# Three attentions of a fused two-block transformer: their steps ordered in pairs on TensorE, ScalarE and VectorE

## The chip, the cores and the metric

The kernel runs on one core of one Trainium2 chip, as one launch. The metric is the device time of that launch in microseconds (us). The core has five engines that run their own instruction streams and meet at semaphores: TensorE (PE; its weight loads are shown apart as PEld), VectorE (DVE), ScalarE (ACT), GpSimd (POOL) and SyncE (SP), which here only issues DMAs.

## What is computed

Two transformer blocks in float32 on one sequence of 512 tokens with a width of 1024. The first has a sparse attention over selected keys (a), a squared-relu MLP, a forgetting attention (b) and a second MLP; the second block has a grouped-query attention (c), an MLP, a chunked gated MLP and a last MLP. Cut to the three attentions, with 16 heads of 64:

```python
# a: keys of each query chosen by an indexer; 4 key/value heads for 16 query heads
p = jax.nn.softmax(jnp.where(valid, q @ k_sel.T * scale, -jnp.inf)); o = p @ v_sel
# b: causal, 16 key/value heads, with a decay added to the scores
p = jax.nn.softmax(jnp.where(causal, q @ k.T * scale + decay, -jnp.inf)); o = p @ v
# c: all 512 keys, 4 key/value heads, normed and rotated queries and keys
p = jax.nn.softmax(q @ k.T * scale); o = p @ v
```

Each o is multiplied by an output weight and added to the residual.

## The kernel before

The program is written engine by engine (`tensor_program`, `scalar_program`, `vector_program`, `gpsimd_program`, `sync_program`), each in the order in which its engine executes it. There is no scheduler: what stands first in a function is issued first, and an engine that waits for a semaphore holds everything written behind it. The activations lie transposed (width on the partitions, tokens along the free dimension). Float32 accuracy in the large matmuls comes from a split of both operands into a high and a low part: `Xhi`, `Xlo` for the activations, `whi`, `wlo` for the weights.

An attention is 32 steps. `STEPS` (line 358) lists them: step n is the pair of heads c = n // 4 and the block of 128 queries i = n % 4. In a and b a block sees only the keys up to its own, so a step's width w is 128, 256, 384 or 512 in turn (`width`, line 362); in c it is always 512. A step has two rows, r = 2n and r = 2n + 1, one for each head. The work of a step, and the lines of it:

- scores (L666, in b with a second product behind it, L674): one product of queries and keys for each head, each in a PSUM bank of its own (`score_bank`: banks 0 to 3, two steps in turn);
- VectorE takes both rows out of PSUM into `PROBS`, with scale or mask and the row's extreme (L1534 in c, L1536 in a and b);
- ScalarE takes the exponential in place and sums it (L1120);
- VectorE inverts both sums of the step (L1549) and multiplies one row in four by its factor (L1552); GpSimd multiplies the other three (L1947);
- turning (L694): TensorE transposes the two rows, in blocks of 64 by 128, into banks 4 and 5;
- the two banks are copied to `TURNED`, of which there are three: of four rows ScalarE copies three (L1114) and VectorE the fourth, row 0 of each even step (L1543);
- values (L711): TensorE multiplies the turned rows with v into bank 6 or 7, one for each pair of heads in turn;
- after four steps the bank holds a chunk of the result; ScalarE writes its high part `Xhi` (L1124), then VectorE the low part `Xlo` (L1556), which waits for `Xhi`. `VALUED` (line 355) says at which n of the loop that is done: 12, 16, 20, ..., 36 and 38.

The steps are staggered. TensorE's loop (`steps`, lines 715 to 722) does at n the scores of n, the turning of n - 4 (`TURN`) and the values of n - 6 (`SUM`). ScalarE's (`attend`, L1103) does at n the copies of turning n - 4 and then both exponentials of n. VectorE's (`attend`, L1519) does at n the score rows of n, at even n the copy of turning n - 4, then the factors of n - 1, and `Xlo`. GpSimd's follows the factors in the order of the steps.

What waits for what, among these: the turning of n waits until both banks of turning n - 1 have been copied (`tr_act`, `tr_dve`), and for its scaled rows (`pn_dve`, `pn_pool`). The scores of n wait until VectorE has taken out the scores of n - 2 (`sc_out`), which had the same banks. The values of n wait for the copies of turning n, and at the first step of a pair of heads also for an earlier `Xlo`, whose bank they reuse (lines 705 and 706). VectorE's score rows of n wait for turning n - 5, which frees their place among the ten rows of `PROBS` (`ROWS`). The first four steps of b are done between the tiles of the product before it, and those of c likewise; the other 28 steps of each attention stand alone. A product with `Xhi` and `Xlo` follows each attention (L531 to L533).

Of the kernel before, what the change touches and what calls it, by code (L numbers as in the profile page):

```python
# [133 lines left out]
def body(nc, ctx, t, consts, out):  # L134
# [289 lines left out]
    def tensor_program(pe):  # L424
# [225 lines left out]
        def attention(a, last, heads_q, heads_k, heads_v):  # L650

            base, x0 = 64 * ATT[a], fill_base(a + "o")[1]
            end = GEMM[last].end

            def scores(n):
                c, i = STEPS[n]
                w = width(a, i)  # L660
                for e in range(2):
                    if TURN <= n < TURN + 2:
                        pe_until.wait_ge(*freed(end - 4 + (score_bank(n, e) - end) % 4))
                    elif n >= 2:
                        pe_until.wait_ge(sc_out, base + 2 * n + e - 3)
                    m = pe.matmul(bank[score_bank(n, e)][:, 0:w], heads_q(2 * c + e, i), heads_k(2 * c + e, w), start=True, stop=(a != "b"))  # L666
                    if a != "b":
                        m.then_inc(sc_full, 1)
                if a == "b":


                    for e in range(2):
                        o, h = 64 * e, 2 * c + e
                        pe.matmul(bank[score_bank(n, e)][:, 0:w], PICK[o:o + 64, h:h + 1].to_broadcast([64, P]), CK[o:o + 64, 0:w],  # L674
                                  start=False, stop=True).then_inc(sc_full, 1)

            def turn(n):

                by_dve, by_pool = scaled_by(a, n)
                if n:  # L680
                    pe_until.wait_ge(pn_dve, by_dve)
                else:
                    pe_until.wait_ge(sc_out, base + 6)
                pe_until.wait_ge(pn_pool, by_pool)
                if n:
                    by_act, by_dve = turned_by(a, 2 * n - 1)
                    pe_until.wait_ge(tr_act, by_act)
                    pe_until.wait_ge(tr_dve, by_dve)
                last = STEPS[n][1] if a != "c" else NT - 1
                for e in range(2):  # L690
                    for j in range(last + 1):
                        for h in range(2):
                            o, at = 64 * h, 256 * e + 64 * j
                            m = pe.transpose(bank[4 + h][:, at:at + 64], PROBS[a][(2 * n + e) % ROWS][o:o + 64, j * P:(j + 1) * P], ident[o:o + 64, o:o + 64])  # L694
                            if e and j == last:
                                m.then_inc(tr_full, 1)

            def values(n):
                c, i = STEPS[n]
                by_act, by_dve = turned_by(a, 2 * n + 1)  # L700
                pe_until.wait_ge(tr_act, by_act)
                pe_until.wait_ge(tr_dve, by_dve)
                if n == 0:
                    pe_until.wait_ge(sc_out, base + 8)
                if c >= 2 and i == 0:
                    pe_until.wait_ge(x_lo, x0 + c - 1)
                blocks = width(a, i) // P
                for j in range(blocks):
                    for e in range(2):
                        at = 256 * e + 64 * j  # L710
                        m = pe.matmul(bank[6 + c % 2][64 * e:64 * e + 64, i * P:(i + 1) * P].rearrange("p (h q) -> p h q", h=2), heads_v(2 * c + e, j),  # L711
                                      TURNED[a][n % 3][:, :, at:at + 64], start=(j == 0), stop=(j == blocks - 1))
                m.then_inc(pv_done, 1)

            def steps(first, to=len(STEPS) + SUM):
                for n in range(first, to):
                    if n < len(STEPS):
                        scores(n)
                    if TURN <= n < len(STEPS) + TURN:
                        turn(n - TURN)  # L720
                    if n >= SUM:
                        values(n - SUM)
            return steps


# [255 lines left out]
    def scalar_program(act):  # L981
# [120 lines left out]

        def attend(a, first=0, to=len(STEPS) + SUM + 1):  # L1103
            base = 64 * ATT[a]
            for n in range(first, to):
                if TURN <= n < len(STEPS) + TURN:
                    w = width(a, STEPS[n - TURN][1])
                    for h in range(2):
                        r = 2 * (n - TURN) + h
                        if r % 4:  # L1110
                            act_until.wait_ge(tr_full, base + r + 1)
                            if r >= 6:
                                act_until.wait_ge(pv_done, 32 * ATT[a] + r // 2 - 2)
                            act.activation(by_heads(TURNED[a][r // 2 % 3][:, h, :], w), by_heads(bank[4 + h][:], w), ACT_F.Copy).then_inc(tr_act, 1)  # L1114
                if n < len(STEPS):
                    w = width(a, STEPS[n][1])
                    for r in (2 * n, 2 * n + 1):
                        p, st = PROBS[a][r % ROWS], stat[:, r % ROWS, :]
                        act_until.wait_ge(sc_out, base + r + 1)
                        act.activation(p[:, 0:w], p[:, 0:w], ACT_F.Exp, bias=st[:, 0:1], scale=-1.0, accum_out=st[:, 1:2]).then_inc(ex_done, 1)  # L1120
                if n in VALUED:
                    c = VALUED[n]
                    act_until.wait_ge(pv_done, 32 * ATT[a] + NT * (c + 1))
                    act.activation(Xhi[:, c, :], bank[6 + c % 2][:], ACT_F.Copy).then_inc(x_hi, 1)  # L1124
# [235 lines left out]
    def vector_program(dve):  # L1360
# [157 lines left out]

        def attend(a, mask):  # L1519
            base, hi0 = 64 * ATT[a], fill_base(a + "o")[0]  # L1520
            for n in range(len(STEPS) + SUM + 1):
                if n < len(STEPS):
                    i = STEPS[n][1]
                    w = width(a, i)
                    for r in (2 * n, 2 * n + 1):
                        p, st = PROBS[a][r % ROWS], stat[:, r % ROWS, :]
                        b = bank[score_bank(n, r % 2)]
                        dve_until.wait_ge(sc_full, base + r + 1)
                        if r >= ROWS:
                            dve_until.wait_ge(tr_full, base + 2 * (n + 1) - ROWS)  # L1530
                        mk = mask(i, w)
                        if mk is None:
                            at = 16 * i + 2 * STEPS[n][0] + r % 2
                            dve.tensor_scalar(p[:, 0:w], b[:, 0:w], RQ[:, at:at + 1], None, ALU.mult, ALU.min, accum_out=st[:, 0:1]).then_inc(sc_out, 1)  # L1534
                        else:
                            dve.tensor_tensor_reduce(p[:, 0:w], b[:, 0:w], mk, -0.125, 3e38, ALU.add, ALU.min, st[:, 0:1]).then_inc(sc_out, 1)  # L1536
                if TURN <= n < len(STEPS) + TURN and (n - TURN) % 2 == 0:
                    r = 2 * (n - TURN)
                    w = width(a, STEPS[n - TURN][1])
                    dve_until.wait_ge(tr_full, base + r + 1)  # L1540
                    if r >= 6:
                        dve_until.wait_ge(pv_done, 32 * ATT[a] + r // 2 - 2)
                    dve.tensor_copy(by_heads(TURNED[a][r // 2 % 3][:, 0, :], w), by_heads(bank[4][:], w)).then_inc(tr_dve, 1)  # L1543
                if 1 <= n < len(STEPS) + 1:
                    w = width(a, STEPS[n - 1][1])
                    r = 2 * n - 2
                    p, both = PROBS[a][r % ROWS], stat[:, r % ROWS:r % ROWS + 2, :]
                    dve_until.wait_ge(ex_done, base + r + 2)
                    dve.reciprocal(both[:, :, 2], both[:, :, 1]).then_inc(rc_done, 1)  # L1549
                    if n % 2 == 0:  # L1550
                        dve_until.wait_ge(rc_done, base // 2 + n)
                        dve.tensor_scalar(p[:, 0:w], p[:, 0:w], both[:, 0, 2:3], None, ALU.mult).then_inc(pn_dve, 1)  # L1552
                if n in VALUED:
                    c = VALUED[n]
                    dve_until.wait_ge(x_hi, hi0 + c + 1)
                    dve.tensor_tensor(Xlo[:, c, :], bank[6 + c % 2][:], Xhi[:, c, :].bitcast(F32), ALU.subtract).then_inc(x_lo, 1)  # L1556
# [580 lines left out]
```

## Time and profile before

| | us |
|---|---|
| median of 3 runs (2575.81 to 2576.2) | 2576.0 |
| span of the profiled execution | 2575.1 |
| TensorE busy | 2537.8 (99%) |
| VectorE busy | 1337.4 (52%) |
| GpSimd busy | 1238.5 (48%) |
| ScalarE busy | 987.1 (38%) |
| DMA queue 1, share of 16 engines | 32.6% |

The profile is of one execution. Its span runs from the first to the last instruction of the program and is 0.9 us under the median of the timed runs; the profiled execution has no other time of its own. In a timeline the instructions of one engine that follow each other and are alike are one row, with x for their number; a row's length then runs from the start of the first to the end of the last. The ends of matmuls are modelled, so starts are the better measure on TensorE. A float32 product of these steps appears as two MATMUL instructions. Neighbouring instructions of VectorE and of ScalarE overlap by up to 0.1 us in the records.

### The profile page before, as it was taken

What the parts mean: (1) busy time and instruction counts of PE and PEld (TensorE: products, weight loads), DVE (VectorE), ACT (ScalarE), POOL (GpSimd) and SP (SyncE); (2) the same over time, 40 slices, a digit from 0 to 9 for tenths busy, and PEclk for the clock granted to TensorE, in tenths of its full rate; (3) what the DMA queues carried; (4) which work ended last, traced back from release to release, by engine and by line L of the source; (5) the groups of instructions that cost most, each with busy time, mean ns of one, the idle gap of its engine ahead of it and who ended that gap; (6) DMA issues with size and microseconds to landing.
All of it is one profiled execution on the core that took longest, in us unless ns stands there. A gap on an engine that the chain in (4) does not pass through costs nothing.

```text
span 2575.1 us, 34368 instructions
## 1 busy us (share of the span) xinstructions
PE 2537.8 (99%) x13922; PEld 2084.2 (81%) x13922; DVE 1337.4 (52%) x2303; ACT 987.1 (38%) x1685; POOL 1238.5 (48%) x609
## 2 busy tenths in 40 slices
PE   8999999999999999999999999999999999999999
PEld 5668888888777888888877888888888888888887
DVE  4884999843236699982875522124345223532121
ACT  4475423224357432233476432223324223432231
POOL 4875444444456444444587444444434434444442
PEclk9999999999999999999999999999999999999999
DMA  4111665532320465542310233333332232333321
GB/s 144 55 34 55 199 196 181 183 111 82 98 82 18 132 195 191 185 152 94 123 42 27 90 98 99 98 98 123 115 98 80 85 99 82 99 98 97 97 96 71
DMA packets 260897, 277.12 MB, mean 108 GB/s; under 512 B 7172, under 2 KB 249476, under 8 KB 260484
## 3 DMA queue, kind: packets, MB, share of 16 engines
q1 hardware_dynamic: 259140, 272.31, 32.6%
q8 instruction: 110, 1.80, 0.3%
q10 hardware_dynamic: 1600, 2.62, 0.3%
q14 instruction: 47, 0.39, 0.0%
HBM read 270.19 MB, written 2.10 MB: 106 GB/s over the span
## 4 chain that ended last, share of the span: by engine, by line
PE 89%; DVE 7%; issue 2%; ACT 1%; POOL 1%; DMA 0%; SPq 0%; ACTq 0%; DVEq 0%
PE bank L531 22%; PE bank L532 21%; PE bank L533 21%; PE bank L666 3%; PE bank L711 2%; DVE acc L1569 2%; PE bank L625 2%; PE bank L626 2%; PE bank L627 2%; PE bank L694 2%; DVE tmp L1604 2%; DVE Hlo L1607 1%; PE bank L550 1%; PE bank L490 1%; PE bank L939 1%
## 5 line engine op out<-in xcount | busy, mean ns | idle before, releaser
L1897 POOL TENSOR_TENSOR wlo<-raw,whi 128x1024 fp32r<-128x1024 f32 (+1 forms) x408 | 991.2, 2449 | 1223.4 <-ACT whi L995 1130.4
L995 ACT ACTIVATE whi<-raw 128x1024 fp32r<-128x1024 f32 (+1 forms) x408 | 405.6, 1041 | 571.5 <-PE bank L533 496.0
L531 PE MATMUL bank<-Xhi,whi 128*128 128x512 f32 (+1 forms) x1568 | 620.4, 396 | 0.0
L532 PE MATMUL bank<-Xlo,whi 128*128 128x512 f32 (+1 forms) x1568 | 611.5, 390 | 0.0
L533 PE MATMUL bank<-Xhi,wlo 128*128 128x512 f32 (+1 forms) x1568 | 610.5, 389 | 0.0
L531 PE MATMUL bank<-Hhi,whi 128*128 128x512 f32 x976 | 381.9, 391 | 0.0
L532 PE MATMUL bank<-Hlo,whi 128*128 128x512 f32 x976 | 380.3, 390 | 0.0
L533 PE MATMUL bank<-Hhi,wlo 128*128 128x512 f32 x976 | 379.7, 389 | 0.0
L531 PEld LDWEIGHTS bank<-Xhi,whi 128*128 128x128 f32 (+1 forms) x1568 | 293.3, 187 | 68.2 <-issue 6.6
L533 PEld LDWEIGHTS bank<-Xhi,wlo 128*128 128x128 f32 (+1 forms) x1568 | 293.4, 187 | 64.0
L532 PEld LDWEIGHTS bank<-Xlo,whi 128*128 128x128 f32 (+1 forms) x1568 | 293.5, 187 | 61.3 <-issue 1.7
L1569 DVE SCALAR_TENSOR_TENSOR acc<-ada,cond,acc 128x256 f32<-128x256 f32 x336 | 272.7, 812 | 12.0
L1403 DVE SCALAR_TENSOR_TENSOR HT<-bank,MOD,HT 128x512 f32<-128x512 f32 x90 | 67.3, 751 | 385.3 <-PE bank L533 365.9
L1604 DVE SCALAR_TENSOR_TENSOR tmp<-tmp 128x512 f32<-128x512 f32 x128 | 134.3, 1049 | 222.5 <-ACT tmp L1136 222.5
L1136 ACT ACTIVATE tmp<-bank 128x512 f32<-128x512 f32 x128 | 76.6, 598 | 411.0 <-PE bank L533 400.0
L533 PEld LDWEIGHTS bank<-Hhi,wlo 128*128 128x128 f32 x976 | 183.3, 188 | 38.6
L531 PEld LDWEIGHTS bank<-Hhi,whi 128*128 128x128 f32 x976 | 183.2, 188 | 37.7
L532 PEld LDWEIGHTS bank<-Hlo,whi 128*128 128x128 f32 x976 | 183.3, 188 | 37.4
L1607 DVE SCALAR_TENSOR_TENSOR Hlo<-tmp,Hhi 128x512 fp32r<-128x512 f32 x128 | 121.1, 946 | 13.6
L1401 DVE TENSOR_TENSOR HT<-bank,HT 128x512 f32<-128x512 f32 x72 | 49.0, 690 | 142.8 <-PE bank L533 142.8
L625 PE MATMUL bank<-whi,Xhi 128*128 128x512 f32 x240 | 94.6, 394 | 0.0
L627 PE MATMUL bank<-whi,Xlo 128*128 128x512 f32 x240 | 93.5, 389 | 0.0
(302 smaller groups left out, 3405.2 us busy)
## 6 DMA issues: line engine op xcount, KB each, us to landing
ada<-in_ada_w SPq DMA_DIRECT2D x48, 1024.0 KB, 5.2
raw<-in_w_up SPq DMA_DIRECT2D x32, 1024.0 KB, 5.3
raw<-in_w_down SPq DMA_DIRECT2D x32, 1024.0 KB, 5.0
raw<-in_mlp_w_in SPq DMA_DIRECT2D x32, 1024.0 KB, 5.3
raw<-in_mlp_w_out SPq DMA_DIRECT2D x32, 1024.0 KB, 5.0
raw<-in_gmlp_w_in SPq DMA_DIRECT2D x24, 1024.0 KB, 5.0
raw<-in_gmlp_w_out SPq DMA_DIRECT2D x12, 1024.0 KB, 5.0
raw<-in_w_in_a SPq DMA_DIRECT2D x8, 1024.0 KB, 5.2
```

The source lines that it names most:

```text
L531: pe.matmul(b[0:rows, :], whi[s][:, c, j:j + rows], hi[:, c, :], start=(c == 0), stop=False)
L532: pe.matmul(b[0:rows, :], whi[s][:, c, j:j + rows], lo[:, c, :], start=False, stop=False)
L533: m = pe.matmul(b[0:rows, :], wlo[s][:, c, j:j + rows], hi[:, c, :], start=False, stop=(c == KC - 1))
L625: pe.matmul(b[:], Xhi[:, c, q * P:(q + 1) * P], hi[:, k, :], start=(c == 0), stop=False)
L627: m = pe.matmul(b[:], Xlo[:, c, q * P:(q + 1) * P], hi[:, k, :], start=False, stop=(c == KC - 1))
L666: m = pe.matmul(bank[score_bank(n, e)][:, 0:w], heads_q(2 * c + e, i), heads_k(2 * c + e, w), start=True, stop=(a != "b"))
L995: act.activation(whi[u % 2][:, c0:c1, 0:k], src[:, c0:c1, 0:k], ACT_F.Copy).then_inc(hi_done, 1)
L1136: act.activation(tmp[v % 2][:], bank[(gm.tile + o) % 4][:], ACT_F.Relu).then_inc(up_q, 1)
L1569: dve.scalar_tensor_tensor(a[:], src[:, c, :], cd[:, c:c + 1], a[:], ALU.mult, ALU.add).then_inc(ada_step, 1)
L1604: dve.scalar_tensor_tensor(r[:], tmp[v % 2][:], 1.0, tmp[v % 2][:], ALU.mult, ALU.mult).then_inc(up_r, 1)
L1607: dve.scalar_tensor_tensor(Hlo[g % 2][:, o, :], r[:], 1.0, Hhi[g % 2][:, o, :].bitcast(F32), ALU.mult, ALU.subtract).then_inc(h_lo, 1)
L1897: pool.tensor_tensor(wlo[u % 2][:, c0:c1, 0:k], src[:, c0:c1, 0:k], whi[u % 2][:, c0:c1, 0:k].bitcast(F32), ALU.subtract).then_inc(lo_done, 1)
```

## The change

TensorE's loop goes by two steps. For an even n it does the scores of n and n + 1, the turning of n - 4, the values of n - 6 and n - 5, then the turning of n - 3. ScalarE and VectorE get orders by two steps as well. GpSimd's and SyncE's programs, all instructions and all semaphores' counts stay as they were; only the order within the three engines is another. The first four steps (n < `TURN`) and what stands around the attentions are unchanged.

```diff
@@ tensor_program, attention @@
             def steps(first, to=len(STEPS) + SUM):
-                for n in range(first, to):
-                    if n < len(STEPS):
-                        scores(n)
-                    if TURN <= n < len(STEPS) + TURN:
+                for n in range(first, min(to, TURN)):
+                    scores(n)
+                for n in range(TURN, to, 2):
+                    for k in (n, n + 1):
+                        if k < len(STEPS):
+                            scores(k)
+                    if n < len(STEPS) + TURN:
                         turn(n - TURN)
                     if n >= SUM:
                         values(n - SUM)
+                        values(n - SUM + 1)
+                    if n < len(STEPS) + TURN:
+                        turn(n - TURN + 1)
@@ scalar_program, attend @@
+            def exps(r):
...
+                act_until.wait_ge(sc_out, base + r + 1)
+                act.activation(p[:, 0:w], p[:, 0:w], ACT_F.Exp, bias=st[:, 0:1], scale=-1.0, accum_out=st[:, 1:2]).then_inc(ex_done, 1)
+
+            def copy_turned(r):
...
+                act_until.wait_ge(tr_full, base + r + 1)
...
+            for n in range(first, min(to, TURN)):
+                exps(2 * n)
+                exps(2 * n + 1)
+            for n in range(TURN, to, 2):
                 if n < len(STEPS):
...
+                    exps(2 * n)
+                if n < len(STEPS) + TURN:
+                    copy_turned(2 * (n - TURN) + 1)
+                if n < len(STEPS):
+                    exps(2 * n + 1)
+                    exps(2 * n + 2)
+                    exps(2 * n + 3)
+                if n < len(STEPS) + TURN:
+                    copy_turned(2 * (n - TURN) + 2)
+                    copy_turned(2 * (n - TURN) + 3)
                 if n in VALUED:
@@ vector_program, attend @@
+            for n in range(TURN):
+                scores_out(n)
+                if n:
+                    factors(n - 1)
+            for n in range(TURN, len(STEPS) + SUM + 1, 2):
                 if n < len(STEPS):
...
+                    scores_out(n)
+                if n < len(STEPS) + TURN:
                     r = 2 * (n - TURN)
...
                     dve.tensor_copy(by_heads(TURNED[a][r // 2 % 3][:, 0, :], w), by_heads(bank[4][:], w)).then_inc(tr_dve, 1)
...
+                if n <= len(STEPS):
+                    factors(n - 1)
+                if n < len(STEPS):
+                    scores_out(n + 1)
+                    factors(n)
                 if n in VALUED:
```

`scores_out` holds the two score rows of a step with their waits, and `factors` the inversion and, at odd steps, the multiply, both with the code that stood in the loop.

TensorE, in the middle of attention c, before (two steps). L666 is scores, L694 turning, L711 values; an x counts products here, not passes:

```order
L666 MATMUL bank<-KC,QC 128x512 x2
L694 MATMUL bank<-ident,PC 128x64 x16
L711 MATMUL bank<-TC,VC 64x128 x8
L666 MATMUL bank<-KC,QC 128x512 x2
L694 MATMUL bank<-ident,PC 128x64 x16
```

and now:

```order
L666 MATMUL bank<-KC,QC 128x512 x4
L694 MATMUL bank<-ident,PC 128x64 x16
L711 MATMUL bank<-TC,VC 64x128 x16
L694 MATMUL bank<-ident,PC 128x64 x16
L666 MATMUL bank<-KC,QC 128x512 x4
```

Scores and values of two steps stand together, with one turning between them on either side.

ScalarE, in the middle of attention c, before, from one `Xhi` on. L1114 is the copy of a turned row, L1120 the exponential of a row, L1124 `Xhi`:

```order
L1124 ACTIVATE Xhi<-bank 128x512
L1114 ACTIVATE TC<-bank 128x512 x2
L1120 ACTIVATE PC,stats<-PC,stats 128x512 x2
L1114 ACTIVATE TC<-bank 128x512
L1120 ACTIVATE PC,stats<-PC,stats 128x512 x2
```

and now, up to an `Xhi` (L1123 copy, L1116 exponential, L1143 `Xhi`):

```order
L1123 ACTIVATE TC<-bank 128x512 x2
L1116 ACTIVATE PC,stats<-PC,stats 128x512
L1123 ACTIVATE TC<-bank 128x512
L1116 ACTIVATE PC,stats<-PC,stats 128x512 x3
L1123 ACTIVATE TC<-bank 128x512 x2
L1143 ACTIVATE Xhi<-bank 128x512
```

The two copies of an odd turning and `Xhi` now stand behind the exponentials of both steps of a pair; before, `Xhi` stood behind those of an even step alone, and the two copies ahead of those of the odd step.

VectorE, in the middle of attention c, before, around one `Xlo`. L1534 is a score row, L1543 the copy of a turned row, L1549 the inversion, L1552 the multiply, L1556 `Xlo`:

```order
L1534 TENSOR_SCALAR PC,stats<-bank,RQ 128x512 x2
L1543 COPY TC<-bank 128x512
L1549 RECIPROCAL stats<-stats 128x2
L1552 TENSOR_SCALAR PC<-PC,stats 128x512
L1556 TENSOR_TENSOR Xlo<-bank,Xhi 128x512
L1534 TENSOR_SCALAR PC,stats<-bank,RQ 128x512 x2
```

and now (L1553 score row, L1580 copy, L1562 inversion, L1565 multiply, L1589 `Xlo`):

```order
L1553 TENSOR_SCALAR PC,stats<-bank,RQ 128x512 x2
L1580 COPY TC<-bank 128x512
L1562 RECIPROCAL stats<-stats 128x2
L1565 TENSOR_SCALAR PC<-PC,stats 128x512
L1553 TENSOR_SCALAR PC,stats<-bank,RQ 128x512 x2
L1562 RECIPROCAL stats<-stats 128x2
L1589 TENSOR_TENSOR Xlo<-bank,Xhi 128x512
L1553 TENSOR_SCALAR PC,stats<-bank,RQ 128x512 x2
```

`Xlo` has moved behind the score rows of the odd step and stands right ahead of those of the next even step; copy, factors and score rows of the odd step keep their order.

## Rows read from the trace of the kernel before

**Rows 1.** The page: span, and busy time of TensorE.
```profile
span 2575.1 us, 34368 instructions
PE 2537.8 (99%) x13922; PEld 2084.2 (81%) x13922; DVE 1337.4 (52%) x2303; ACT 987.1 (38%) x1685; POOL 1238.5 (48%) x609
```

**Rows 2.** Busy time by stretch: attention a, attention c (start:end us, length, engines).
```profile
147.30:212.40 65.10, 60.65 (x769) 42.23 (x769) 48.09 (x199) 57.52 (x185) 50.80 (x48) 0.97 0.01 2
...
1304.40:1394.50 90.10, 86.87 (x1176) 61.96 (x1176) 72.11 (x202) 77.22 (x186) 76.30 (x48) 0.98 0.04 12
```

**Rows 3.** Timeline of TensorE in c (start us, length us, engine, line).
```profile
1343.90 1.13 PE L666 MATMUL bank<-KC,QC 64*128 64x512 f32 x4
1344.87 0.66 PE L694 MATMUL bank<-ident,PC 64*128 64x64 f32 x16
1345.45 1.09 PE L711 MATMUL bank<-TC,VC 128*64 128x128 f32 x16
1346.48 1.13 PE L666 MATMUL bank<-KC,QC 64*128 64x512 f32 x4
```

**Rows 4.** Timeline of TensorE in a, one period of four steps.
```profile
179.02 1.13 PE L666 MATMUL bank<-KA,QA 64*128 64x512 f32 x4
...
186.67 1.13 PE L666 MATMUL bank<-KA,QA 64*128 64x512 f32 x4
```

**Rows 5.** Timeline of TensorE at the start of c; then a stretch's busy times, PEclk.
```profile
1309.45 2.85 PE L666 MATMUL bank<-KC,QC 64*128 64x512 f32 x12
1312.13 0.68 PE L694 MATMUL bank<-ident,PC 64*128 64x64 f32 x16
1312.64 1.08 PE L666 MATMUL bank<-KC,QC 64*128 64x512 f32 x4
1316.14 1.12 PE L694 MATMUL bank<-ident,PC 64*128 64x64 f32 x16 [2.41 <-DVE TC L1543]
...
1316.10:1319.40 3.30, 3.26 (x32) 2.16 (x33) 2.31 (x7) 2.80 (x7) 3.30 (x3) 0.50 0.00 0
```

**Rows 6.** Timeline of VectorE in c.
```profile
1341.27 0.69 DVE L1543 COPY TC<-bank 128x512 f32<-128x512 f32 x1
...
1342.06 0.49 DVE L1552 TENSOR_SCALAR PC<-PC,stats 128x512 f32<-128x512 f32 x1
1342.49 0.75 DVE L1534 TENSOR_SCALAR_CACHE_REDUCE PC<-bank,RQ 128x512 f32<-128x512 f32 x1
...
1343.17 0.75 DVE L1534 TENSOR_SCALAR_CACHE_REDUCE PC<-bank,RQ 128x512 f32<-128x512 f32 x1
```

**Rows 7.** Timeline of ScalarE in c.
```profile
1342.98 1.08 ACT L1114 ACTIVATE TC<-bank 128x512 f32<-128x512 f32 x2 [0.36 <-PE bank L694]
1343.95 0.72 ACT L1120 ACTIVATE PC<-PC,stats 128x512 f32<-128x512 f32 x1
...
1344.66 0.72 ACT L1120 ACTIVATE PC<-PC,stats 128x512 f32<-128x512 f32 x1
```

**Rows 8.** Timeline at the end of c, where a turning waits for ScalarE.
```profile
1384.15 1.09 ACT L1114 ACTIVATE TC<-bank 128x512 f32<-128x512 f32 x2 [0.35 <-PE bank L694]
...
1385.38 0.71 PE L694 MATMUL bank<-ident,PC 64*128 64x64 f32 x16 [0.24 <-ACT TC L1114]
```

**Rows 9.** Timeline of ScalarE and VectorE in a, around one Xlo.
```profile
184.08 0.59 ACT L1124 ACTIVATE Xhi<-bank 128x512 fp32r<-128x512 f32 x1
...
184.70 0.69 DVE L1556 TENSOR_TENSOR Xlo<-bank,Xhi 128x512 fp32r<-128x512 f32 x1 [0.73 <-ACT Xhi L1124]
```

**Rows 10.** Instructions of a by form, 154 to 204 us (busy us, mean ns, idle before).
```profile
L1536 DVE CUSTOM_DVE_ANT_0 PA<-bank,MA 128x384 f32<-128x384 f32 x14 | 7.1, 549 | 1.4 <-PE bank L666 1.3
...
L1120 ACT ACTIVATE PA<-PA,stats 128x256 f32<-128x256 f32 x14 | 7.0, 503 | 2.8 <-DVE stats L1536 2.8
...
L1536 DVE CUSTOM_DVE_ANT_0 PA<-bank,MA 128x256 f32<-128x256 f32 x14 | 5.3, 416 | 0.0
L1114 ACT ACTIVATE TA<-bank 128x256 f32<-128x256 f32 x14 | 4.6, 390 | 0.0
```

More of the change, by code:

```diff
@@ L1104, in attend @@
             base = 64 * ATT[a]
[L1105 to L1114, printed above, removed]
-                if n < len(STEPS):
[L1116 to L1120, printed above, removed]
+            def exps(r):
+                w = width(a, STEPS[r // 2][1])
+                p, st = PROBS[a][r % ROWS], stat[:, r % ROWS, :]
+                act_until.wait_ge(sc_out, base + r + 1)
+                act.activation(p[:, 0:w], p[:, 0:w], ACT_F.Exp, bias=st[:, 0:1], scale=-1.0, accum_out=st[:, 1:2]).then_inc(ex_done, 1)
@@ new lines, in copy_turned @@
+            def copy_turned(r):
+                w, h = width(a, STEPS[r // 2][1]), r % 2
+                act_until.wait_ge(tr_full, base + r + 1)
+                if r >= 6:
+                    act_until.wait_ge(pv_done, 32 * ATT[a] + r // 2 - 2)
+                act.activation(by_heads(TURNED[a][r // 2 % 3][:, h, :], w), by_heads(bank[4 + h][:], w), ACT_F.Copy).then_inc(tr_act, 1)
+            for n in range(first, min(to, TURN)):
+                exps(2 * n)
+                exps(2 * n + 1)
@@ L1520, in attend, with scores_out @@
             base, hi0 = 64 * ATT[a], fill_base(a + "o")[0]
-            for n in range(len(STEPS) + SUM + 1):
-                if n < len(STEPS):
[L1523 to L1537, printed above, removed]
+            def scores_out(n):
+                i = STEPS[n][1]
+                w = width(a, i)
+                for r in (2 * n, 2 * n + 1):
+                    p, st = PROBS[a][r % ROWS], stat[:, r % ROWS, :]
+                    b = bank[score_bank(n, r % 2)]
+                    dve_until.wait_ge(sc_full, base + r + 1)
+                    if r >= ROWS:
+                        dve_until.wait_ge(tr_full, base + 2 * (n + 1) - ROWS)
+                    mk = mask(i, w)
+                    if mk is None:
+                        at = 16 * i + 2 * STEPS[n][0] + r % 2
+                        dve.tensor_scalar(p[:, 0:w], b[:, 0:w], RQ[:, at:at + 1], None, ALU.mult, ALU.min, accum_out=st[:, 0:1]).then_inc(sc_out, 1)
+                    else:
+                        dve.tensor_tensor_reduce(p[:, 0:w], b[:, 0:w], mk, -0.125, 3e38, ALU.add, ALU.min, st[:, 0:1]).then_inc(sc_out, 1)
@@ new lines, in factors @@
+            def factors(n):
+                w = width(a, STEPS[n][1])
+                r = 2 * n
+                p, both = PROBS[a][r % ROWS], stat[:, r % ROWS:r % ROWS + 2, :]
+                dve_until.wait_ge(ex_done, base + r + 2)
+                dve.reciprocal(both[:, :, 2], both[:, :, 1]).then_inc(rc_done, 1)
+                if n % 2:
+                    dve_until.wait_ge(rc_done, base // 2 + n + 1)
+                    dve.tensor_scalar(p[:, 0:w], p[:, 0:w], both[:, 0, 2:3], None, ALU.mult).then_inc(pn_dve, 1)
@@ L1543, in attend @@
                     dve.tensor_copy(by_heads(TURNED[a][r // 2 % 3][:, 0, :], w), by_heads(bank[4][:], w)).then_inc(tr_dve, 1)
[L1544 to L1552, printed above, removed]
+                if n <= len(STEPS):
[3 more added lines that the diff above has]
+                    factors(n)
                 if n in VALUED:
```

## Prediction, made before the changed kernel ran

> **What bounds the kernel now.** I read the page first. TensorE is busy for 2537.8 of 2575.1 us [rows 1], so the question is only where TensorE's own order leaves time, or will leave it. The change touches the three attentions alone, a, b and c. Attention a takes 65.1 us and c 90.1 us of the span [rows 2], b about as long as a. In c, ScalarE is busy 77.2 us and GpSimd 76.3 us: neither is far behind TensorE's 86.9.
>
> Then TensorE's timeline in c. From one step's scores to the next one's are 2.58 us (1343.90 to 1346.48): scores 0.97, turning 0.58, values 1.03 [rows 3]. No row has an idle time, so a step is bound by TensorE, and two steps take 5.16 us. Attention a repeats every four steps, from one 512-wide score at 179.02 to the next at 186.67: 7.65 us, or 3.83 for two steps [rows 4].
>
> **What the change takes from TensorE.** Nothing is added or removed, every matmul stays; fewer changes of kind remain. Three steps of scores in a row (12 passes) took 1312.13 - 1309.45 = 2.68 us, and a first one costs 0.97, so a further one costs (2.68 - 0.97) / 2 = 0.85. A turning with scores behind it took 1312.64 - 1312.13 = 0.51 instead of 0.58 [rows 5]. Two steps as the change orders them are then scores 2 x 0.85, turning 0.58, values about 1.03 + 0.87 (16 more passes at the pitch within the block), turning 0.56 (0.51 and a slower first pass after values): 4.74 us against 5.16. That is 0.4 us per pair, and with 14 pairs in each of three attentions 17 us, if TensorE alone decides. The Trainium skill, page "TensorEngine Tiling (Array Packing)", section "Key Properties", says that changing the tiling mode, and not merely the tile, drains TensorE. By that rule scores and turning (both 64 rows) follow each other free and the change removes two of four drains per pair; by it the time would be near 2559. The rows of a turning (0.51 before scores, 0.58 before values) agree in sign.
>
> **What it does to the others.** This is where I expect the time to go. Let n be an even step. In one pass of the new loop VectorE does: both score rows of n, copy of turning n-4, factors of n-1, both score rows of n+1, factors of n, and every fourth step Xlo. ScalarE does: exponential, copy, then three exponentials (the last two are of step n+1), then both copies of turning n-3, and every fourth step Xhi. TensorE does scores n and n+1, turning n-4, values n-6 and n-5, turning n-3; turning n-2 of the next pass waits until both copies of turning n-3 have emptied banks 4 and 5.
>
> This closes a ring, which I follow in c from the first score row of n+1 on VectorE:
> - its row takes 0.75 until ScalarE may start (VectorE's 512-wide row) [rows 6];
> - two exponentials 2 x 0.71 (1343.95 to 1344.66), two copies 1.08, or 0.97 up to the start of what follows them (1342.98 to 1343.95) [rows 7];
> - from the copies' end at 1385.23 to turning at 1385.38 0.15, the turning 0.71, for whose end VectorE's copy waits [rows 8];
> - copy and reciprocal 0.79 (1341.27 to 1342.06), multiply 0.43 (to 1342.49), where the first score row of n+3 starts [rows 6].
>
> Sum 0.75 + 1.42 + 1.08 + 0.15 + 0.71 + 0.79 + 0.43 = **5.33 us** for two steps: already more than 5.16, and TensorE's 4.74 no longer matters. Before, the copies of a turning stood ahead of the exponentials on ScalarE, and this ring did not exist.
>
> Every fourth step it is worse. Xlo on VectorE waits for Xhi on ScalarE; such a wait is in a already (0.73 us, Xhi 0.59, Xlo starts 0.03 after it [rows 9]). Now Xhi stands behind two more exponentials and two more copies, and both score rows of n+2 are queued behind Xlo. The ring then reads: row 0.75, exponentials 1.42, copies up to the next start 0.97, Xhi 0.59, 0.03, Xlo 0.69 less 0.08 of overlap, both score rows of n+2 1.35, copy and reciprocal 0.79, multiply 0.43 = **6.94 us**. Turning n-2 is done by then, so it adds nothing.
>
> Between the score rows of steps 5 and 31 lie 13 such intervals; Xlo stands in 5 of them (n = 12, 16, 20, 24, 28). Attention c: 8 x 5.33 + 5 x 6.94 = 77.3 us, before 13 x 5.16 = 67.1: **+10.2**.
>
> Attention a has widths of 128 to 512. From 256 to 512 the ring holds a 256-wide score row (0.42), two exponentials (0.50 each) and two copies (0.39 each) [rows 10]: 0.33, 2 x 0.22 and 2 x 0.20 less than at 512. Its 12-pass turning, 384-wide copy and 256-wide multiply save about 0.12 to 0.14 each, in proportion. That gives 5.33 - 1.58 = 3.75, and with Xlo, where the two score rows are 384 wide (0.55 each [rows 10]), 5.2. From 512 back to 256 the turning has 4 passes and the copy is 128 wide: 5.33 - 0.06 - 0.37 - 0.40 = 4.5. The 13 intervals are 2 x 3.75 + 5 x 5.2 + 6 x 4.5 = 60.5 us; before 13 x 3.83 = 49.8: **+10.7**. Attention b has the same widths, but its scores need a further pass on TensorE, which lengthened its steps before and hardly lengthens the ring; I take **+9.8**.
>
> The tails. After step 31 turnings and values remain. Turning 30 now waits for both copies of turning 29 (1.08 + 0.15), the values of step 28 for an Xlo that stands behind them, and the values of step 31 for the copies of turning 31 with only one block of values to cover them. I take +3 in c and +2.4 in a and in b, **+7.8** together; the bounds are 0 (all waits there before too) and 4 each. The start, up to the score rows of step 5, has the same order on VectorE, whose work fills it, and costs nothing.
>
> GpSimd keeps its order; its three multiplies per pair fit into 5.33, and it runs ahead. No DMA moves. What follows the attentions is only shifted, with its cover unchanged.
>
> Sum: 10.2 + 10.7 + 9.8 + 7.8 = 38.5 us. Against the profiled execution: 2575.1 + 38.5 = 2613.6 of span, and with the 0.9 us by which the median of 2576.0 stands over that span, 2614.5, rounded to **2615 us** (+1.5%).
>
> **Rivals.**
> - *TensorE stays the bound.* For it: it is busy without a gap now, and 4.74 per pair would hold if copies and exponentials overlapped. Against it: the ring above, each link of which is an order within one engine or a wait in the code. It would give 2576 - 17 = 2559 us.
> - *The ring holds, but Xlo costs nothing extra*, if Xhi and Xlo find room. Then c has 13 x 5.33 = 69.3 (+2.2), a 7 x 3.75 + 6 x 4.5 = 53.3 (+3.5), b +2.6, tails +7.8: 16.1 in all, 2592 us. Against it: VectorE's order has the score rows behind Xlo.
> - *The clock falls too.* With TensorE waiting up to 1.7 us in a pass, its clock may fall, as it did in c: after TensorE had stood still, a stretch of 3.3 us had a granted clock of 0.50, the lower of its two levels [rows 5]. If each of the 39 turnings in the ring were lengthened from 0.71 to 1.12, as the one at 1316.14 was [rows 5], 16 us come on top: 2631 us. The Trainium skill, page "TensorE: Matmul & The Clock Gate", section "HAM oscillation — how this bites in real kernels", warns of such falls where TensorE idles between bursts. Against it: TensorE would still be busy for more than two thirds of each stretch.
> - *No change*: ring and gain cancel, 2576 us. It would need a ring of 5.16 in c without Xlo's part; nothing speaks for it.
>
> **How the numbers follow.** Forecast 0.75, the clock 0.10, ring without Xlo's cost 0.07, TensorE the bound 0.06, no change 0.02. The range is that of the forecast and of the clock: the low end 2603 has tails at 0 and some 4 us less in the rings (the length of a row taken for a wait), the high end 2633 is the clock's case and 2 us. What is left out is 0.15 and a little. A measurement of this kernel tells 0.2%, some 5 us, from no change: faster 0.06, same 0.02, slower 0.92.
>
> **What would show it.** In the timeline of c after the change: no 2.58 us rhythm, but score rows of odd steps on VectorE 5.3 and 6.9 us apart by turns; TensorE idle before a turning, released by ScalarE's copy; VectorE idle for over 2 us before every Xlo, released by Xhi; in a 4.5 and 5.2. The three attentions together are 39 us longer, and everything else is as long as before. If score blocks follow each other 4.7 us apart with no idle time, I am wrong, and the drain rule was all that mattered. If VectorE's wait for Xhi is short, it is the second rival; if turnings take 1.1 us in the steady stretch, the third.

## The result, and the profile after

| | us |
|---|---|
| before, median of 5 runs (2575.81 to 2578.2) | 2576.2 |
| changed, median of 5 runs (2628.98 to 2632.31) | 2631.75 |
| ratio, 95% interval | 1.0212, 1.0200 to 1.0223 |
| span of the changed kernel's profiled execution | 2627.6 |

The change makes the kernel 2.1% slower. The forecast was 2615 us, 1.5%, with 2603 to 2633 as its range.

The page of the changed kernel, to be read against [rows 1]:

```profile
span 2627.6 us, 34368 instructions
PE 2552.9 (97%) x13922; PEld 2100.0 (80%) x13922; DVE 1330.2 (51%) x2303; ACT 990.9 (38%) x1685; POOL 1244.1 (47%) x609
```

The same 13922 matmuls. TensorE is busy 15 us longer for them, and idle 37 us more. By stretch, attention a, attention c, then the tail of a and the tail of b (from the score rows of step 31 to the next product; after the five engines' busy times stands the granted clock), against [rows 2]:

```profile
147.30:232.20 84.90, 67.73 (x767) 50.30 (x764) 46.83 (x199) 58.97 (x184) 52.39 (x48) 0.84 0.01 2
...
1343.30:1447.10 103.80, 87.33 (x1176) 61.50 (x1176) 69.60 (x202) 77.27 (x186) 79.09 (x48) 0.98 0.03 10
...
218.80:232.20 13.40, 9.41 (x124) 7.71 (x124) 3.87 (x12) 6.31 (x16) 5.13 (x4) 0.75 0.00 1
848.90:863.20 14.30, 10.52 (x124) 8.79 (x124) 3.87 (x12) 6.32 (x16) 5.15 (x4) 0.64 0.01 1
```

Attention a takes 84.9 us instead of 65.1, c 103.8 instead of 90.1. In c TensorE has its old busy time, 87.3 us, and only waits more. In a it is busy 67.7 instead of 60.7 us for the same instructions: its granted clock was 0.84 there, and before it was 0.97.

VectorE in c, around one `Xlo`. Lines are the changed kernel's: L1553 score row, L1580 copy, L1562 inversion, L1565 multiply, L1589 `Xlo`:

```profile
1389.51 0.74 DVE L1553 TENSOR_SCALAR_CACHE_REDUCE PC<-bank,RQ 128x512 f32<-128x512 f32 x1
...
1393.30 0.69 DVE L1589 TENSOR_TENSOR Xlo<-bank,Xhi 128x512 fp32r<-128x512 f32 x1 [2.29 <-ACT Xhi L1143]
1393.91 0.74 DVE L1553 TENSOR_SCALAR_CACHE_REDUCE PC<-bank,RQ 128x512 f32<-128x512 f32 x1
...
1395.25 0.68 DVE L1580 COPY TC<-bank 128x512 f32<-128x512 f32 x1
...
1396.04 0.49 DVE L1565 TENSOR_SCALAR PC<-PC,stats 128x512 f32<-128x512 f32 x1
1396.44 0.74 DVE L1553 TENSOR_SCALAR_CACHE_REDUCE PC<-bank,RQ 128x512 f32<-128x512 f32 x1
```

and ScalarE in the same stretch (L1116 exponential, L1123 copy, L1143 `Xhi`):

```profile
1390.30 0.72 ACT L1116 ACTIVATE PC<-PC,stats 128x512 f32<-128x512 f32 x1 [0.66 <-DVE PC L1553]
...
1391.73 1.06 ACT L1123 ACTIVATE TC<-bank 128x512 f32<-128x512 f32 x2
1392.68 0.59 ACT L1143 ACTIVATE Xhi<-bank 128x512 fp32r<-128x512 f32 x1
```

This is the ring with `Xlo`, link by link: score row at 1389.51, exponentials from 1390.30, copies from 1391.73, `Xhi` from 1392.68, `Xlo` at 1393.30 after a wait of 2.29 us, and the first score row of the next odd step at 1396.44: 6.93 us. TensorE waits where the ring passes it (L694 turning, L711 values, L666 scores):

```profile
1390.67 1.94 PE L666 MATMUL bank<-KC,QC 64*128 64x512 f32 x8
1392.93 0.71 PE L694 MATMUL bank<-ident,PC 64*128 64x64 f32 x16 [0.32 <-ACT TC L1123]
1394.05 1.97 PE L711 MATMUL bank<-TC,VC 128*64 128x128 f32 x32 [0.41 <-DVE Xlo L1589]
1396.25 0.72 PE L694 MATMUL bank<-ident,PC 64*128 64x64 f32 x16 [0.23 <-ACT TC L1123]
1396.77 2.28 PE L666 MATMUL bank<-KC,QC 64*128 64x512 f32 x8
1399.86 0.34 PE L694 MATMUL bank<-ident,PC 64*128 64x64 f32 x4 [0.81 <-ACT TC L1123]
```

In c the intervals between the first score rows of odd steps from 13 on are 6.9 and 5.3 us by turns. Below, an interval is always the time from the first score row of one odd step to that of the next, so it holds one pair of steps. Each attention can be cut at the score rows of step 5 and step 31 (us, read from the starts in the two traces):

| | a before | a after | b before | b after | c before | c after |
|---|---|---|---|---|---|---|
| step 5 to step 31 | 49.2 | 64.9 | 51.3 | 65.2 | 67.1 | 77.8 |
| step 31 to the next product | 9.1 | 13.5 | 9.1 | 14.4 | 10.9 | 13.9 |

### The profile page after: what moved, and what is told of

Read it like the earlier page. It is cut to its first block, busy times and chain, and to the rows that moved or that the text cites. A ratio compares the mean times of both kernels' runs of the same rounds, so it can differ in the third digit from the quotient of the medians.

```text
span 2627.6 us, 34368 instructions
## 1 busy us (share of the span) xinstructions
PE 2552.9 (97%) x13922; PEld 2100.0 (80%) x13922; DVE 1330.2 (51%) x2303; ACT 990.9 (38%) x1685; POOL 1244.1 (47%) x609
## 4 chain that ended last, share of the span: by engine, by line
PE 84%; DVE 9%; ACT 4%; issue 3%; POOL 0%; DMA 0%; SPq 0%; ACTq 0%; DVEq 0%
PE bank L531 21%; PE bank L532 21%; PE bank L533 21%; DVE acc L1602 2%; PE bank L625 2%; PE bank L626 2%; PE bank L627 2%; PE bank L711 2%; DVE tmp L1637 1%; PE bank L694 1%; PE bank L666 1%; DVE Hlo L1640 1%; PE bank L550 1%; PE bank L490 1%; PE bank L945 1%
## 5 line engine op out<-in xcount | busy, mean ns | idle before, releaser
L533 PEld LDWEIGHTS bank<-Hhi,wlo 128*128 128x128 f32 x976 | 183.3, 188 | 38.5
```

The costliest lines, as they stand in the source:

```text
L533: m = pe.matmul(b[0:rows, :], wlo[s][:, c, j:j + rows], hi[:, c, :], start=False, stop=(c == KC - 1))
```

## The experiments

Eight kernels ran, in two groups, each group beside runs of the kernel before. Their diffs are against the changed kernel unless said otherwise. A ratio is to the kernel before:

| | median us | ratio | 95% interval |
|---|---|---|---|
| e1, `Xhi` early | 2615.0 | 1.0152 | 1.0137 to 1.0167 |
| e2, copies ahead | 2610.0 | 1.0126 | 1.0110 to 1.0143 |
| e3, both | 2573.3 | 0.9986 | 0.9977 to 0.9995 |
| e4, TensorE's order alone | 2590.3 | 1.0054 | 1.0039 to 1.0069 |
| e5, e1 with scores again | 2603.3 | 1.0104 | 1.0091 to 1.0118 |
| e6, changed with scores again | 2623.7 | 1.0185 | 1.0170 to 1.0201 |
| e7, e3 with another tail | 2571.6 | 0.9985 | 0.9977 to 0.9994 |
| e8, e3 without TensorE's pairs | 2586.7 | 1.0035 | 1.0022 to 1.0047 |

### e1: Xhi early

```diff
                 if n < len(STEPS):
                     exps(2 * n + 1)
+                if n in VALUED:
+                    ...
+                    act.activation(Xhi[:, c, :], bank[6 + c % 2][:], ACT_F.Copy).then_inc(x_hi, 1)
+                if n < len(STEPS):
                     exps(2 * n + 2)
                     exps(2 * n + 3)
                 if n < len(STEPS) + TURN:
                     copy_turned(2 * (n - TURN) + 2)
                     copy_turned(2 * (n - TURN) + 3)
-                if n in VALUED:
-                    ...
```

> The changed kernel with one edit on ScalarE: Xhi stands right behind the second exponential of the even step, ahead of the odd step's exponentials and copies, so that VectorE need not wait for it. Ring theory: every interval between odd steps' score rows in c is 5.33 us, none 6.95; c loses 5 x 1.6 = 8 us against the changed kernel, a and b 7 each and about 1 each in their tails: near 2606 us, 2600 to 2610, less if TensorE's clock also falls less. Rival (the time lies in TensorE's clock and its idling, and Xlo's wait is only where it shows): Xlo's wait goes, the intervals stay near 12.3 us for four steps, over 2622 us.

Measured 2615.0 us, 5 above the upper end that I gave. In c it came out as the ring says: all intervals after the first are 5.3 us, 69.6 us from step 5 to 31 instead of 77.8. VectorE's timeline in c of e1, score row to score row (1380.26 to 1385.60, 5.34 us) with no `Xlo` wait between:

```profile
1380.26 0.75 DVE L1554 TENSOR_SCALAR_CACHE_REDUCE PC<-bank,RQ 128x512 f32<-128x512 f32 x1
...
1382.54 0.75 DVE L1554 TENSOR_SCALAR_CACHE_REDUCE PC<-bank,RQ 128x512 f32<-128x512 f32 x1 [0.78 <-PE bank L666]
...
1384.40 0.69 DVE L1581 COPY TC<-bank 128x512 f32<-128x512 f32 x1 [0.43 <-PE bank L694]
...
1385.60 0.75 DVE L1554 TENSOR_SCALAR_CACHE_REDUCE PC<-bank,RQ 128x512 f32<-128x512 f32 x1
```

In a nothing was gained, and in b 0.6 us: a takes 65.3 us, with intervals of 4.5 and 5.8 by turns where the ring gives 4.5 and 3.75. The stretches of TensorE's busy times in a of e1 show why: two neighbouring stretches and the whole.

```profile
183.00:186.40 3.40, 3.40 (x32) 2.64 (x30) 1.36 (x7) 2.05 (x7) 2.60 (x3) 0.54 0.02 5
186.40:193.00 6.60, 5.29 (x70) 3.62 (x68) 4.31 (x19) 5.19 (x17) 3.70 (x4) 1.00 0.00 0
160.00:215.00 55.00, 47.19 (x510) 34.96 (x512) 31.16 (x133) 40.51 (x127) 36.28 (x33) 0.83 0.01 2
```

TensorE's timeline in the same place of e1:

```profile
181.78 0.34 PE L694 MATMUL bank<-ident,PA 64*128 64x64 f32 x4 [1.30 <-ACT TA L1123]
182.05 2.68 PE L711 MATMUL bank<-TA,VA 128*64 128x128 f32 x28
```

In each period of 10.3 us TensorE waits for ScalarE's copies (1.30 us at 181.78), and after that there is a stretch with a granted clock of 0.54, close to the lower of its two levels, in which values and turning take longer: 28 passes of values 2.68 us. What `Xhi` gave back the clock took. Whether the clock is the cause or the mark is what e5 asks.

### e2: copies ahead

```diff
                 if n < len(STEPS):
                     exps(2 * n + 1)
+                if n < len(STEPS) + TURN:
+                    copy_turned(2 * (n - TURN) + 2)
+                    copy_turned(2 * (n - TURN) + 3)
+                if n < len(STEPS):
                     exps(2 * n + 2)
                     exps(2 * n + 3)
-                if n < len(STEPS) + TURN:
-                    copy_turned(2 * (n - TURN) + 2)
-                    copy_turned(2 * (n - TURN) + 3)
```

> The changed kernel with one other edit on ScalarE: the two copies of the odd turning stand ahead of the odd step's two exponentials; Xhi stays last. Ring theory: the copies no longer wait for the exponentials, so the plain interval in c falls from 5.33 to TensorE's 4.75, and the one with Xlo from 6.95 by the two copies to about 5.97; four steps 10.7 in c (before the change 10.3), about 8.0 in a (before 7.65). Near 2583 us, 2575 to 2592. Rival (the order of values and turning on TensorE costs, whatever ScalarE does): over 2600 us.

Measured 2610.0 us, 27 above what I expected of it. The plain intervals of c fell to 4.9 and 4.3 us, so the copies' ring is open. The interval with `Xlo` did not fall to 5.97 but rose to 7.5. A timeline of c in e2 has the link that I left out:

```profile
1377.10 0.59 ACT L1144 ACTIVATE Xhi<-bank 128x512 fp32r<-128x512 f32 x1
1377.72 0.69 DVE L1590 TENSOR_TENSOR Xlo<-bank,Xhi 128x512 fp32r<-128x512 f32 x1 [2.88 <-ACT Xhi L1144]
...
1378.47 1.97 PE L711 MATMUL bank<-TC,VC 128*64 128x128 f32 x32 [1.52 <-DVE Xlo L1590]
...
1380.66 0.71 PE L694 MATMUL bank<-ident,PC 64*128 64x64 f32 x16 [0.23 <-ACT TC L1123]
...
1381.38 1.08 ACT L1123 ACTIVATE TC<-bank 128x512 f32<-128x512 f32 x2 [0.27 <-PE bank L694]
```

With the copies ahead of the exponentials, ScalarE first waits for the odd turning, which TensorE does only after both values; the exponentials and `Xhi` come after that, `Xlo` after `Xhi`, VectorE's next score rows after `Xlo`, and TensorE's next values wait for `Xlo` too (1.52 us). I had taken the copies' time out of the ring and not put the odd turning's in. The edit breaks one ring and lengthens the other. In a the granted clock fell as well, to 0.91 from step 5 to step 31 and to 0.53 in the tail; no run separates what share of the 27 us that is.

### e3: both

```diff
                 if n < len(STEPS):
                     exps(2 * n + 1)
+                if n in VALUED:
+                    ...
+                if n < len(STEPS) + TURN:
+                    copy_turned(2 * (n - TURN) + 2)
+                    copy_turned(2 * (n - TURN) + 3)
+                if n < len(STEPS):
                     exps(2 * n + 2)
                     exps(2 * n + 3)
-                if n < len(STEPS) + TURN:
-                    ...
-                if n in VALUED:
-                    ...
```

> The changed kernel with both edits on ScalarE: Xhi right behind the even step's exponentials, then the copies of the odd turning, then the odd step's exponentials. Ring theory: nothing on ScalarE or VectorE stands in a ring longer than TensorE's work, so two steps take TensorE's 4.75 us in c and about 3.5 in a and b; c 5 us, a and b 4 us each under the kernel before, the tails up to 3 over: near 2565 us, 2560 to 2574, and the clock falls nowhere but where it fell before. Rival (GpSimd or VectorE, each with 4.4 to 4.7 us of work for two steps, becomes the bound): 2574 to 2585.

Measured 2573.3 us, faster than the kernel before by 0.14% (0.9977 to 0.9995), at the end of what I expected of the ring theory. The two edits are worth 17 us (e1) and 22 us (e2) alone and 58 us together. In c TensorE now runs by its own work, one pair in e3:

```profile
1341.19 1.94 PE L666 MATMUL bank<-KC,QC 64*128 64x512 f32 x8
1342.96 0.66 PE L694 MATMUL bank<-ident,PC 64*128 64x64 f32 x16
1343.55 1.97 PE L711 MATMUL bank<-TC,VC 128*64 128x128 f32 x32
1345.45 0.71 PE L694 MATMUL bank<-ident,PC 64*128 64x64 f32 x16
1345.99 0.65 PE L666 MATMUL bank<-KC,QC 64*128 64x512 f32 x2
```

1341.19 to 1345.99 is 4.80 us, against 5.16 in [rows 3] for the same products. In a four steps take 4.14 + 3.23 = 7.37 us instead of 7.65. From step 5 to 31 e3 is 1.5, 1.4 and 3.8 us shorter than before in a, b and c, but its tails in a and c are 2.0 and 1.7 longer.

### e4: TensorE's order alone

Against the kernel before, the changed kernel's `steps` and nothing else.

```diff
-                for n in range(first, to):
...
+                for n in range(TURN, to, 2):
+                    for k in (n, n + 1):
...
```

> TensorE's order alone: TensorE as in the changed kernel, ScalarE and VectorE as in the kernel before. Ring theory: ScalarE's copies of the odd turning stand ahead of the odd step's exponentials here too, so the long ring is absent; but Xlo stands ahead of the odd step's score rows on VectorE, which now has little slack, and costs up to 1 us in four steps. Near 2572 us, 2563 to 2582. Rival (TensorE's order is what costs): near the changed kernel, over 2610.

Measured 2590.3 us, 8 above the upper end I gave. The rival is refuted: with the old orders on ScalarE and VectorE about three quarters of the loss is gone (14 us are left of 55). But `Xlo` costs more than the 1 us in four steps that I allowed: four steps of c take 6.9 + 4.3 = 11.2 us, 1.7 over the 9.5 of TensorE's pairs. VectorE's timeline in c of e4 (L1562 `Xlo`):

```profile
1360.68 0.69 DVE L1562 TENSOR_TENSOR Xlo<-bank,Xhi 128x512 fp32r<-128x512 f32 x1 [1.34 <-ACT Xhi L1130]
1361.29 0.74 DVE L1540 TENSOR_SCALAR_CACHE_REDUCE PC<-bank,RQ 128x512 f32<-128x512 f32 x1
```

### e5 and e6: more work for TensorE

Both repeat the scores of the steps of width 128 and 256 in a and b, three times in all, into the same banks; e5 on e1, e6 on the changed kernel.

```diff
+            def again(n):
+                return 3 if a != "c" and n >= 6 and STEPS[n][1] < 2 else 1
...
+                for rep in range(again(n)):
+                    for e in range(2):
+                        if rep:
+                            m = pe.matmul(bank[score_bank(n, e)][:, 0:w], heads_q(2 * c + e, i), heads_k(2 * c + e, w), start=True, stop=(a != "b"))
...
```

> The kernel of e1 with idle TensorE time filled: in attentions a and b, from step 6 on, the scores of the steps of width 128 and 256 are computed three times into the same banks, with the same result; nothing else is changed, and c not at all. In e1 the intervals of a alternate between 4.5 us, as forecast, and 5.8 us where the ring gives 3.75, and the granted clock is 0.5 in a stretch of 3.4 us in every period of some 10 us. Clock theory: the excess of 2 us is TensorE at its lower clock; with more work for it the clock stays up, and the interval falls to 3.8 to 4.3 us although TensorE does more: 10 us less in a and 5 to 8 in b, near 2600 us. Rival (the excess is some wait of the ring that I left out, and the clock only a mark of idling): the interval stays at 5.8 or grows, 2615 us or more.

> The changed kernel with the same filling of TensorE in a and b. Ring theory with the clock as the rest of the forecast's miss: rings of a and b as forecast, 60.5 us from step 5 to step 31 instead of 64.9 and 65.2, tails by 1 to 3 us shorter if the clock holds there: near 2620 us, 2615 to 2625. Rival (the clock has no part in it): 2632 us or more.

e5 measured 2603.3 us, 12 less than e1, with more instructions on TensorE. The same stretch of a as in e1, in e5:

```profile
160.00:215.00 55.00, 49.55 (x676) 38.61 (x676) 35.73 (x155) 46.34 (x145) 42.03 (x39) 1.00 0.01 2
```

The clock is 1.00 instead of 0.83, and the intervals are 4.2 and 4.5 us. The 28 passes of values that took 2.68 us in e1 take, in TensorE's timeline of e5:

```profile
179.40 0.34 PE L703 MATMUL bank<-ident,PA 64*128 64x64 f32 x4 [0.44 <-ACT TA L1132]
179.67 1.75 PE L720 MATMUL bank<-TA,VA 128*64 128x128 f32 x28
...
183.21 0.53 PE L703 MATMUL bank<-ident,PA 64*128 64x64 f32 x12
```

The edit only adds matmuls; it takes away no wait and changes no order. So the 1.6 us by which the interval fell, from 5.75 to 4.16, are the clock's, and with them the 9.6 us of a, which takes 55.7 us here from step 5 to step 31 and 65.3 in e1. The 0.4 us that are left over the ring's 3.75 are a link that the ring does not have: TensorE has no wait from its turning at 179.40 to that at 183.21, with two blocks of values and two of scores between them, none of them a repeated one. The changed kernel too has an interval of 4.16 there (step 9 to step 11, at a clock of 1.00).

e6 measured 2623.7 us, 8 less than the changed kernel. The stretches of a and b from step 5 to 31 in e6:

```profile
154.00:215.00 61.00, 52.22 (x712) 40.26 (x712) 38.16 (x163) 47.27 (x153) 44.18 (x41) 1.00 0.01 2
779.80:840.90 61.10, 57.02 (x812) 46.73 (x812) 38.21 (x162) 46.87 (x149) 43.39 (x41) 1.00 0.01 2
```

They are 60.4 and 61.1 us long between the score rows themselves, against 64.9 and 65.2. With the clock held up, a takes what the forecast had, 60.5, but two errors of its intervals cancel in that sum: the five with `Xlo` are 5.1 us instead of 5.2, and one of the two plain ones is 4.16 instead of 3.75. The time of e6 would be lower still if the clock had not fallen in the tail of c, which took 17.1 us in its profile instead of 13.9; nothing was changed there.

### e7: e3 with another tail

TensorE's loop by single steps from step 32 on, against e3:

```diff
-                for n in range(TURN, to, 2):
+                for n in range(TURN, min(to, len(STEPS)), 2):
...
+                for n in range(len(STEPS), to):
+                    if n < len(STEPS) + TURN:
+                        turn(n - TURN)
+                    values(n - SUM)
```

> The kernel of e3, with TensorE's order by single steps from step 32 on, where only turnings and values are left; ScalarE and VectorE have the same order there in either case. Theory: the tails of e3 (11.1, 9.3 and 12.5 us from the score rows of step 31 on) are long because two values stand ahead of an odd turning; by single steps they are as before the change, 9.1, 9.1 and 10.9: 3 to 4 us less than e3, near 2570 us, and faster than both kernels. Rival (the tails are long because step 31 is reached sooner, and GpSimd or the copies end them): no change against e3, 2573.

Measured 2571.6 us, ratio 0.9985 (0.9977 to 0.9994), and e3's interval is the same: the timed runs do not tell the two apart. The profiles do in part. The tail of c in e3, then in e7:

```profile
1381.05 0.71 PE L694 MATMUL bank<-ident,PC 64*128 64x64 f32 x16 [1.26 <-ACT TC L1123]
...
1383.58 0.71 PE L694 MATMUL bank<-ident,PC 64*128 64x64 f32 x16
1385.55 0.71 PE L694 MATMUL bank<-ident,PC 64*128 64x64 f32 x16 [1.26 <-ACT TC L1123]
```

```profile
1379.28 0.71 PE L694 MATMUL bank<-ident,PC 64*128 64x64 f32 x16 [1.26 <-ACT TC L1124]
...
1381.28 0.71 PE L694 MATMUL bank<-ident,PC 64*128 64x64 f32 x16 [0.26 <-DVE PC L1567]
...
1383.22 0.71 PE L694 MATMUL bank<-ident,PC 64*128 64x64 f32 x16 [0.21 <-ACT TC L1124]
```

In pairs two turnings stand side by side and the second waits 1.26 us for the copies of the first; e3 has that twice, e7 once, and with values between two turnings the wait is 0.2 to 0.3 us. The tails are 9.4, 9.3 and 11.6 us in e7, 11.1, 9.3 and 12.5 in e3. In the tail of a the granted clock was 0.85 in e3 and 1.00 in e7 as well, and no run tells the order's share from the clock's there. Both are faster than the kernel before and than the changed one; e7 is the better of the two in its profile only.

### e8: e3 without TensorE's pairs

TensorE's `steps` of the kernel before in e3.

```diff
-                for n in range(TURN, to, 2):
...
+                for n in range(first, to):
+                    if n < len(STEPS):
+                        scores(n)
...
```

> The kernel of e3 with TensorE's order by single steps throughout, as before the change, under the orders of ScalarE and VectorE of e3. Theory: what e3 gains is TensorE's, by fewer changes of kind; here two steps of c take 5.15 us again and the time is that of the kernel before, 2574 to 2580. Rival (e3 gains by its places of Xhi and Xlo or by the order on ScalarE): 2573 as e3, with TensorE's steps at 4.8.

Measured 2586.7 us, 7 above the upper end that I gave. In c it is as expected, 5.2 us for two steps, without idle time on TensorE, and the rival is refuted. In a it is worse than expected: 4.2 + 4.1 = 8.3 us for four steps, with short waits of TensorE for copies and for GpSimd. The orders of e3 fit TensorE's pairs better than its single steps: the pairs are worth 13 us under them and cost 14 us under the old ones (e4).

## Why the forecast was right in direction and short in size

By its own steps; the spans of the two profiled executions are 52.5 us apart, the sum had 38.5.

- **TensorE's own gain.** Forecast 4.74 us for a pair in c; measured 4.80 where nothing else binds (e3). Right; the difference is in the scores of two steps, 1.77 us (1341.19 to 1342.96) where the sum had 1.70. The Trainium skill, page "TensorEngine Tiling (Array Packing)", section "Key Properties", says that a change of tiling mode drains TensorE. The trace agrees with that in sign: a pair takes 0.36 us less with fewer changes of mode, though no run here separates the drain from the rest of that gap. That TensorE's own gain decides the kernel's time was the first rival, and it is refuted: in the changed kernel the gain is covered by waits.
- **The ring of copies.** 5.33 us forecast in c, 5.34 measured (e1), and 5.3 in every plain interval of the changed kernel after the first, which is 5.7 (5.5 before). Right. e3 shows the cause: with copies and `Xhi` moved, all of it goes.
- **The wait for `Xhi`.** 6.94 forecast, 6.93 measured; c took 77.8 us from step 5 to 31 where the forecast had 77.3. Right, and the second rival (no cost for `Xlo`) is refuted by e1, which took it out.
- **a and b.** Forecast 60.5 us for a; measured 64.9, and 60.4 in e6, where the repeated scores held the clock up. For b the +9.8 us had no rows behind it, and e6 has 61.1 - 51.3 = 9.8: that it fits so well is in part luck. Here the step failed that left the clock's case out of the sum: "TensorE would still be busy for more than two thirds of each stretch" was given as a reason against it. It was busy for 82% of a's stretch, and the clock fell all the same, to 0.87 on average:

```profile
153.80:218.80 65.00, 53.38 (x618) 38.66 (x618) 37.52 (x163) 47.14 (x149) 43.58 (x41) 0.87 0.01 2
783.60:848.90 65.30, 54.69 (x668) 41.95 (x669) 37.67 (x163) 47.31 (x149) 43.42 (x41) 0.92 0.01 2
```

  A clock that stays up and one that falls stand side by side in a of the changed kernel, cut here at 186 us:

```profile
158.00:186.00 28.00, 22.22 (x298) 16.02 (x294) 17.18 (x76) 21.51 (x70) 19.70 (x18) 0.99 0.01 2
186.00:218.80 32.80, 27.11 (x290) 19.99 (x290) 17.91 (x77) 22.66 (x71) 19.97 (x19) 0.79 0.01 2
```

  In the first stretch both intervals with `Xlo` are 5.1 us and the ones from 512 back to 256 are 4.5, as forecast; in the second the three with `Xlo` are 5.8 to 6.7 us.

  The third rival, ring and clock together, was given 2631 us and a chance of 0.10; it is what happened. Its pricing was not right in its places: it put 0.41 us on each of 39 turnings, but in c the clock stayed up, while in a and b whole stretches of values and scores were slowed too. So it is luck that its 2631 us lies so near the measured 2631.75, and the range, whose upper end of 2633 was taken from that rival, holds the result by 1.25 us.
- **Tails.** +2.4, +2.4 and +3 us forecast; +4.4, +5.3 and +3.0 measured. In c, at a clock of 1.00, the sum held, but in part by luck. The three waits that the forecast named are there (1.26 us before turning 30, 0.41 before the values of step 28, and a short one in those of step 31), but the longest one it did not name, in TensorE's timeline of the changed kernel:

```profile
1436.67 0.71 PE L694 MATMUL bank<-ident,PC 64*128 64x64 f32 x16 [2.90 <-ACT TC L1123]
```

  This is turning 28, which waits for the copies of turning 27; they stand behind both exponentials of step 31, and no scores are left to cover them. In a and b the granted clock was 0.75 and 0.64. No run shows the tails of this order at 1.00 (e5, with `Xhi` early, had 1.00 in that of b, which took 10.9 us). In e6 they had 0.87 and took 13.0 and 12.8 us, and the 28 passes of values in them took 3.18 and 2.94 us where e5 has 1.75 in the middle of a. An estimate from these numbers: with such a block at the full clock either tail would take 11.6 us, and the forecast had 9.1 + 2.4 = 11.5.

So, with stretches read to 0.1 us, 13.7 us of the 52.5 are c, near the forecast (13.2). 19.9 are a and 19.2 are b, where 13.1 and 12.2 were forecast. In e6, 4.5 us of a's excess and 4.1 of b's are gone between steps 5 and 31; what is in their tails (2 to 3 us each) was not separated by a run.

Where did TensorE's 17 us go when the rings were open (e3, e7)? The profiled span of e7 is 6.3 us under that of the kernel before. In c 3.8 of the 5.5 expected between steps 5 and 31 arrived, since pairs take 4.9 us in the first half and 4.80 later, not 4.74. In a and b about 1.4 of about 5 each arrived. TensorE's weight loads for the scores wait for VectorE's score rows there, for 1.6 us in 40 us of e7, but the kernel before has 0.9 of that too, so it does not account for what is missing. Why a and b gain so little stays open; no run has tried it.

## What to carry to other kernels

When one engine's order is coarsened to save its own overhead, follow each engine's new order once round: add the links from one point back to the same point, and compare that ring with the time of the engine that bounds. Each edit to the order of a helper engine should be weighed with the others, since here neither of two edits recovered half of the loss and both together recovered all of it. Where the bounding engine is made to wait in short pieces, look at its granted clock before pricing the rest of its work, and count its tail separately.

## What was not expected of the hardware

TensorE's granted clock fell although TensorE was busy most of the time: in e1, with waits of 1.30 us in every 10.3 us and TensorE busy 47.2 of 55 us, the clock averaged 0.83, and 28 passes of values took 2.68 us where they took 1.75 in e5. In c, with waits of 0.3, 0.4 and 0.8 us and TensorE busy 10.5 of 12.4 us, it stayed at 1.00:

```profile
1387.00:1399.40 12.40, 10.49 (x144) 7.33 (x144) 8.68 (x27) 9.59 (x24) 10.07 (x7) 1.00 0.01 2
```

What sets the two stretches apart was not tried, and the same waits did not always bring the fall: in a of the changed kernel TensorE waits up to 1.30 us at a time both before and after 186 us, with a clock of 0.99 and then of 0.79; in the tail of c it waits 2.90 and 1.26 us both in the changed kernel and in e6, with 1.00 in the one and 0.80 in the other. Adding matmuls whose results are not needed made the changed kernel 8 us faster (e6) and e1 12 us faster (e5).
